# Attention stage of an MLA and mLSTM trunk: where one matmul of a score sum and one multiply of q stand in their engines' queues

## The reference, cut to what matters

```
q = (rms_norm(c_q, g_q) @ w_uq)   # 16 heads x (64 + 32 rotary)
kv = (rms_norm(c_kv, g_kv) @ w_ukv)
for blk in range(4):
    s = (q_n @ k_n + q_r @ k_r) * scale       # keys up to the block's end
    s = where(k_idx <= q_idx, s, -inf)
    p = softmax(s)
    outs.append(p @ v)
```

## Time and profile before

| | us |
|---|---|
| median of 3 runs (lowest, highest) | 1299.8 (1299.15, 1300.79) |
| the profiled execution | 1299.99 |
| its span in the profile | 1298.2 |
| PE busy (share of the span) | 1231.2 (95%) |
| DVE busy | 675.5 (52%) |
| ACT busy | 455.1 (35%) |
| POOL busy | 281.1 (22%) |
| mean granted TensorE clock | 0.975 |

### The profile page before, as it was taken

How to read it: one execution, slowest core, us unless ns; L and a number is a source line. 1 busy time by engine, 2 the same in 40 slices (tenths; PEclk the granted TensorE clock), 3 DMA queues, 4 the chain that set the end, 5 groups by cost and what they waited for, 6 DMA issues and landing times.

```text
span 1298.2 us, 15828 instructions
## 1 busy us (share of the span) xinstructions
PE 1231.2 (95%) x5829; PEld 1016.0 (78%) x5829; DVE 675.5 (52%) x958; ACT 455.1 (35%) x725; POOL 281.1 (22%) x252
## 2 busy tenths in 40 slices
PE   6889999899999999999999998889999999999997
PEld 5667777678888888888889986676888888888885
DVE  6867888744533434434457544974443343343432
ACT  4336666543212212222343235652322221221232
POOL 4222222222201102002112134552220020110211
PEclk8999999899999999999999998988999999999998
DMA  5201011222233332232233331011323223223221
GB/s 159 60 22 28 23 26 25 94 68 94 97 98 97 98 97 97 97 97 97 67 99 99 113 97 47 27 41 38 99 91 102 94 97 100 94 97 97 97 66 65
DMA packets 113888, 104.00 MB, mean 80 GB/s; under 512 B 20935, under 2 KB 112165, under 8 KB 113837
## 3 DMA queue, kind: packets, MB, share of 16 engines
q1 hardware_dynamic: 113344, 102.98, 25.1%
q10 hardware_dynamic: 492, 0.31, 0.1%
HBM read 101.17 MB, written 2.11 MB: 80 GB/s over the span
## 4 chain that ended last, share of the span: by engine, by line
PE 79%; DVE 8%; issue 6%; ACT 3%; POOL 2%; ACTq 0%; DMA 0%; DVEq 0%; POOLq 0%
PE ps L1466 24%; PE ps L1468 24%; PE ps L1467 24%; DVE nmax L1109 2%; POOL xl L568 1%; DVE xl L968 1%; DVE qtmp L1101 1%; ACT prob L712 1%; ACT uh L726 1%; DVE rinv L1114 1%; ACT whi L636 1%; DVE diag L1382 1%; ACT xh L698 0%; PE ps L1716 0%; PE ps L1717 0%
## 5 line engine op out<-in xcount | busy, mean ns | idle before, releaser
L963 DVE TENSOR_TENSOR wlo<-raw,whi 128x2048 fp32r<-128x2048 f32 (+2 forms) x89 | 194.4, 2188 | 157.3 <-ACT whi L636 157.3
L1466 PE MATMUL ps<-xl,whi 128*128 128x512 f32 (+1 forms) x688 | 270.7, 393 | 3.2 <-DVE krot L1048 3.2
L636 ACT CAST whi<-raw 128x2048 fp32r<-128x2048 f32 (+4 forms) x150 | 184.7, 1259 | 246.3 <-PE ps L1468 237.7
L1467 PE MATMUL ps<-xh,whi 128*128 128x512 f32 (+1 forms) x688 | 268.5, 390 | 0.0
L1468 PE MATMUL ps<-xh,wlo 128*128 128x512 f32 (+1 forms) x688 | 268.3, 390 | 0.0
L1466 PE MATMUL ps<-ul,whi 128*128 128x512 f32 x608 | 237.2, 390 | 1.2 <-POOL wlo L516 1.2
L1468 PE MATMUL ps<-uh,wlo 128*128 128x512 f32 x608 | 236.6, 389 | 0.0
L1467 PE MATMUL ps<-uh,whi 128*128 128x512 f32 x608 | 236.5, 389 | 0.0
L546 POOL TENSOR_TENSOR ul<-sq,uh 128x512 fp32r<-128x512 f32 x64 | 83.7, 1309 | 521.1 <-ACT uh L815 521.1
L1191 DVE TENSOR_TENSOR h<-ps,h 128x512 f32<-128x512 f32 x80 | 55.0, 690 | 199.3 <-PE ps L1468 192.6
L1466 PEld LDWEIGHTS ps<-xl,whi 128*128 128x128 f32 (+1 forms) x688 | 128.9, 187 | 32.0 <-issue 4.9
(11 more groups left out here) (234 smaller groups left out, 1648.0 us busy)
## 6 DMA issues: line engine op xcount, KB each, us to landing
raw<-in_mlp_w SPq DMA_DIRECT2D x64, 1024.0 KB, 5.1
raw<-in_mlstm_w_in SPq DMA_DIRECT2D x12, 1024.0 KB, 5.3
raw<-in_mla_w_o SPq DMA_DIRECT2D x4, 1024.0 KB, 5.0
raw<-in_mlstm_w_o SPq DMA_DIRECT2D x4, 1024.0 KB, 5.0
raw<-in_mla_w_in SPq DMA_DIRECT2D x3, 1024.0 KB, 5.4
raw<-in_mla_w_uq SPq DMA_DIRECT2D x16, 192.0 KB, 2.5
x_tok<-in_x SPq DMA_DIRECT2D x4, 512.0 KB, 5.6
mb<-m_rows SPq DMA_DIRECT2D x8, 256.0 KB, 3.4
```

The lines of the kernel that those rows point to most:

```text
L636: last = sc.copy(hi, src)
L963: last = v.tensor_tensor(lo, src, hi.bitcast(F32), ALU.subtract)
L1466: mm(o, ah, bl, start=first, stop=False)
L1467: mm(o, ah, bh, start=False, stop=False)
```

## The change

Three edits of order; every instruction stays, with its operands and shape.

1. `scores` is split. `scores_high` issues q high x k low, q high x k high and now the mask product; `scores_low` waits for `q_lo` (b = 0), issues q low x k high as the last of the sum, and raises `s_mm`.
2. For block 0 of lead 1 `scores_low` stands behind `k_product`, and for block 0 of lead 2 behind the second part of `weigh(i, 0)`. Elsewhere the two halves follow each other directly.
3. On DVE, `q_table(i, 1)` stands ahead of `normalise(i, 0, 2)`.

```diff
@@ DVE, attention(i)
                 pt_low(i, 0, 0)
+                q_table(i, 1)
                 normalise(i, 0, 2)
-                q_table(i, 1)
                 row_max(i, 0, 3)
@@ PE
-            def scores(i, lead, b):
+            def scores_high(i, lead, b):
...
                 mm(o, qh[e][:, part], kh[e][:, 0:w], start=False, stop=False)
+                mm(ps[:, B_S + b % 2, P * b:w], identr[:], maskr[:], start=False, stop=False)
+
+            def scores_low(i, lead, b):
+
+                e, w = lead % 2, P * (b + 1)
                 if b == 0:
                     pe.wait_ge(q_lo, i * 2 + (lead + 1))
-                mm(o, ql[e][:, part], kh[e][:, 0:w], start=False, stop=False)
-                mm(ps[:, B_S + b % 2, P * b:w], identr[:], maskr[:], start=False, stop=True).then_inc(s_mm, 1)
+                mm(ps[:, B_S + b % 2, 0:w], ql[e][:, P * b:P * b + P], kh[e][:, 0:w], start=False, stop=True) \
+                    .then_inc(s_mm, 1)
+
+            def scores(i, lead, b):
+
+                scores_high(i, lead, b)
+                scores_low(i, lead, b)
@@ PE, attention(i)
                 turn_p(i, 0, 2)
-                scores(i, 1, 0)
+                scores_high(i, 1, 0)
                 if not last:
                     strip_ready(N_PAIR + 2, i, 2)
                     pe.wait_ge(k_lo, i * 2 + 2)
                     k_product(N_PAIR % 2)
+                scores_low(i, 1, 0)
                 turn_p(i, 0, 3)
...
                 if not last:
-                    scores(i, 2, 0)
+                    scores_high(i, 2, 0)
                 weigh(i, 0, (1,))
+                if not last:
+                    scores_low(i, 2, 0)
```

## The result

| | before | changed |
|---|---|---|
| median of 12 runs each, in turns (us) | 1298.8 | 1307.1 |
| ratio (95% interval) | | 1.0072 (1.0054 to 1.0090) |
| profiled execution, its span (us) | 1299.99, 1298.2 | 1306.24, 1304.4 |

The change makes the kernel slower by 0.72%, which is 1.0072 x 1298.8 - 1298.8 = 9.4 us, with 7.0 to 11.7 as the interval. The forecast was +10.2 us and 1310.0. It was reckoned from 1299.8; on that base the measured ratio gives 1309.2 us, inside the range of 1307.5 to 1314.0. The bare median of 1307.1 belongs to a set of runs in which the kernel before came out 1.0 us lower than 1299.8.

A forecast was written before the change was run, and what follows sets the result against it. The prediction took the chain of waits over DVE and ACT to pace the attention loop, with PE following. Six delays of 1.70 us, +0.1 in pair 0 and -0.1 in pair 7 gave 1299.8 + 10.2 = 1310.0 us, range 1307.5 to 1314.0.

The forecast's parts named there:

- What paces the loop: Attention stage, pairs 1 to 6: DVE and ACT pace the softmax loop, period 20.75 us; PE, nearly full, follows it.
- The k product's place: PE, pairs 1 to 6: the k product still waits for POOL's strip and starts at 184.04, so PE gains nothing ahead.
- The delay per pair: Head 1's block 0, pairs 1 to 6: DVE's row maximum starts at 185.90 instead of 184.20, 1.70 us later.
- lower bound of 1.64: Least delay in us of head 1's block 0 maximum, from a product of this shape that took 0.27 without waiting.
- Slack behind it: DVE and ACT behind the late maximum: no idle piece absorbs the 1.70 us, so six periods give 10.2 us.
- Pair 0 and pair 7: First and last pair of the attention stage: +0.1 us from one more 128-column product, -0.1 from the table multiply.
- The table multiply: q's multiply moved ahead on DVE: zero; rival, 0.07 together with overlooked slack: 0.54 us gained in eight pairs, 1305.7.
- Late strip: Rival, 0.05: q's low part precedes POOL's second piece, delaying strip and k product up to 0.69 us each, 1314.
- The clock: Rival, 0.06: PE's two new holes lower its clock, k products take up to twice 1.50 us, 1319 at most.
- The sum: Whole kernel: 10.2 + 0.1 - 0.1 = 10.2 us on 1299.8, giving 1310.0; forecast's chance 0.74.

The follow-up runs named there:

- behind the weighing alone: Kernel before with lead 2's low product of block 0 behind the weighing's second part, mask product ahead of the low product in every block; ratio 1.0024 to before.
- v's rounding: Kernel before with ACT's rounding of v, which releases POOL's v part, behind the rounding of block 3's probabilities instead of ahead; ratio 0.9942 to before.
- the table multiply alone: Kernel before with only q's table multiply moved on DVE, ahead of the normalise of block 2; ratio 1.0004 to before.
- q's chain forward: Kernel before with v's rounding later, q's table multiply and low part earlier on DVE, and q's rounding earlier on ACT; ratio 0.9978 to before.

## Why the prediction was right

- **What paces the loop.** Right, and shown from both sides: a wait of PE's taken away gave nothing (behind the weighing alone), and 0.80 us of blocked DVE time taken away gave all of it (v's rounding). The count of 141 pieces in the chain is that of the view from 183 to 205 us; from one maximum to the next it is 136, none of them PE's.
- **The k product's place.** Right: it starts with POOL's strip, 189.45 and 189.51, and PE's hole of 0.87 us turned into 1.21 in front of the k product.
- **The delay per pair.** Mis-sized by 0.10. I gave the low product the 0.33 us of the one that had waited. In the stream behind 512-column products it takes 0.22. The delay was 1.60 instead of 1.70, and six times 0.10 is 0.6 us too much. This is most of the 0.8 us between forecast and result. My lower bound of 1.64 was too high as well, for the same reason: it came from a product that stood behind short ones. The prediction's own range, 1308.5 to 1312, went below its six delays of 1.64 (1309.6) without a term for it.
- **Slack behind it.** None, as put. DVE's 0.81 us hole and the long multiply (1.07 us) moved along whole.
- **Pair 0 and pair 7.** Pair 0 gave +0.06 from k product to k product, for +0.1; the clock was low in part of it in both profiles, so the agreement says little. For pair 7, the time from head 1's first maximum in pair 6 to the end of the long wait in pair 7 fell from 25.08 to 24.82 us, and to 24.85 with the table multiply alone: -0.25 for -0.1. There no strip of POOL's stands beside q's low part.
- **The table multiply.** The term of zero was right, one step under it was not. I wrote that ACT's rounding of q and the next exponential would not move. Against ACT's exponential of block 2, the rounding started 1.96 us behind before and 1.84 with the multiply moved, and the next exponential 2.36 behind instead of 2.56. ACT had waited a little on the table multiply, so the premise of a row without a gap was wrong. The term was zero by its other reason, POOL's second piece. The sign that the 0.54 us hole would turn up again ahead of q's low part came in part only: the hole there is 0.1 us, the low part's own row grew by 0.27.
- **Late strip.** It did not come, by a small margin: in the changed kernel POOL's second piece starts at 187.44 and q's low part at 187.50. Before and after, the strip takes 2.71 us and the low part of q is the one that waits.
- **The clock.** It stayed at 1.00 in the steady pairs of the changed kernel. The rival was a real one: in the kernel with q's chain forward, where PE waited 1.57 us for the strip instead of 1.21, it did fall in one steady pair, and stayed at 1.00 in the others. What singled that pair out is open.
- **The sum.** In the profiles 6 x 1.60 + 0.06 - 0.25 = 9.4, against 9.33 from the first k product to the end of the long wait. That the ratio gives 9.4 as well is closer than its interval of 7.0 to 11.7 can vouch for.

## What to carry to other kernels

An engine that is 92% busy need not pace its loop: look whether the chain of waits enters it at all before filling its holes, and look again behind every gain, for the next limit can be that engine. When a matmul that closes a sum is put behind others to fill a wait, ask whether those others wait for something later still, and who reads the sum; here both answers were bad in one place and harmless in the other. Where DVE was held up by POOL, it did not show as idle time but as a long instruction; comparing the same shape at two places found 0.80 us a pair, which one line moved on another engine gave back.

## What the runs showed of the hardware

- An instruction of DVE with both inputs in SBUF that was issued while POOL ran did not end earlier for being issued earlier. Its record just got longer: 1.23 us, or 1.50 when issued 0.28 us sooner against POOL, with the same end. The Trainium skill (SBUF — State Buffer, "Who interferes with whom") says that the one that comes second blocks for the whole instruction, and the trace agrees: 0.55 us from the end of POOL's piece to its own, against 0.68 for the whole instruction undisturbed.
- The multiply that took 1.09 us instead of 0.29 is of another kind, with one tensor as input and a factor per row, so the prediction's sentence on two inputs in SBUF does not cover it; that POOL holds it up too is measured by itself, with v's rounding moved. It ended at 187.76, 0.07 us behind POOL's v part.
- The same 128-column product took 0.33 us behind a wait, 0.27 behind short products and 0.22 behind 512-column ones. The ends of matmuls are modelled in this profile, but DVE bears the last one out: its maximum started 191.27 - 191.01 = 0.26 us behind the start of the product. A length from a row holds only for a place of the same kind.
